# Nine 512-column strips of a hybrid diffusion layer, computed by seven quarter products

## The reference

```
h = modulate(rms_norm(x))                      # (tokens, 1024)
q, k, v, r = h@Wq, h@Wk, h@Wv, h@Wr            # widths 512, 512, 1024, 1024: gated linear attention (GLA)
o, _ = gla_chunked(q, k, v, decay, state)      # both directions, 4 heads
ya = (rms_norm(o) * silu(r)) @ gla_proj        # 1024 x 1024
yb = Re(DFT2(h @ Wu)) @ fnet_proj              # Fourier mixing
yc = ssd(...) @ ssd_proj                       # Mamba-2 branch, done before q
y  = sigmoid(h@Wga)*ya + sigmoid(h@Wgb)*yb + sigmoid(h@Wgc)*yc
x1 = x + gate * (y @ w_out);  then routed_moe(...)   # 16 experts, top 2
```

## Time and profile before

| | us |
|---|---|
| median of 3 timed runs | 1718.51 |
| lowest, highest | 1715.67, 1721.17 |
| span of the profiled execution | 1712.4 |
| PE busy in it | 1602.6 (94%) |
| DVE busy in it | 691.1 (40%) |
| ACT busy in it | 388.0 (23%) |

### The profile page before, as it was taken

The page is one execution under the profiler, slowest core; times in us unless marked ns, Lnnn a source line. Parts: engine busy times, 40 slices in busy tenths (PEclk is TensorE's granted clock), DMA queues, the critical chain, the costliest instruction groups (busy, mean ns, idle before and its releaser), DMA issues.

```text
span 1712.4 us, 23396 instructions
## 1 busy us (share of the span) xinstructions
PE 1602.6 (94%) x9120; PEld 872.7 (51%) x9121; DVE 691.1 (40%) x1281; ACT 388.0 (23%) x730; POOL 290.2 (17%) x311
## 2 busy tenths in 40 slices
PE   6999999999999899999999999999999979999893
PEld 3464564564554444445455554446575655555451
DVE  2445745745645746000167773033243232222224
ACT  4332432422432310000133334101110211111112
POOL 0006406407407400000000000000000032222222
PEclk9999999999999999999999999999999999999997
DMA  9802301311411574211111012126135269997994
GB/s 344 323 21 81 99 31 44 99 38 37 123 49 25 181 259 150 98 51 49 49 50 49 1 50 84 63 74 238 61 136 197 103 241 392 360 373 283 395 342 159
DMA packets 110339, 248.47 MB, mean 145 GB/s; under 512 B 5665, under 2 KB 15142, under 8 KB 110274
## 3 DMA queue, kind: packets, MB, share of 16 engines
q1 hardware_dynamic: 86800, 180.60, 29.4%
q0 software_dynamic: 14288, 48.96, 7.9%
q10 hardware_dynamic: 9186, 18.01, 3.7%
HBM read 225.40 MB, written 22.15 MB: 145 GB/s over the span
## 4 chain that ended last, share of the span: by engine, by line
PE 81%; DVE 9%; DMA 3%; ACT 2%; issue 2%; POOL 2%; ACTq 0%; DVEq 0%; POOLq 0%
PE psum L456 17%; PE psum L470 9%; PE psum L1152 9%; PE psum L803 6%; PE psum L669 5%; PE psum L1177 5%; PE psum L460 4%; DVE arena L1941 2%; PE psum L969 2%; PE psum L926 2%; PE psum L939 2%; PE psum L850 2%; PE psum L712 1%; PE psum L568 1%; PE psum L703 1%
## 5 line engine op out<-in xcount | busy, mean ns | idle before, releaser
L456 PE MATMUL psum<-arena 128*128 128x512 f32 x688 | 300.8, 593 | 1.3 <-DVE arena L1952 0.8
L456 PEld LDWEIGHTS psum<-arena 128*128 128x128 f32 x688 | 128.1, 189 | 157.4 <-issue 155.9
L1152 PE MATMUL psum<-arena 128*32 128x256 f32 x2816 | 164.5, 385 | 1.5 <-issue 1.0
L470 PE MATMUL psum<-arena 128*128 128x512 f32 x352 | 152.9, 593 | 1.6 <-issue 1.6
L1152 PEld LDWEIGHTS psum<-arena 128*32 128x32 f32 x2816 | 92.7, 110 | 57.9 <-issue 4.9
L669 PE MATMUL psum<-arena 128*128 128x512 f32 x256 | 118.4, 594 | 0.0
L803 PE MATMUL psum<-arena 128*128 128x512 f32 x256 | 111.5, 593 | 0.0
L470 PEld LDWEIGHTS psum<-arena 128*128 128x128 f32 x352 | 66.2, 190 | 81.5 <-issue 81.1
L2416 POOL TENSOR_TENSOR arena<-arena 128x512 f32<-128x512 f32 x64 | 89.3, 1416 | 35.7 <-ACT arena L1469 35.7
L1821 DVE SCALAR_TENSOR_TENSOR arena<-arena 128x772 f32<-128x772 f32 (+1 forms) x96 | 93.9, 978 | 3.4
L2378 POOL TENSOR_TENSOR arena<-arena 128x512 f32<-128x512 f32 x40 | 44.9, 1130 | 277.7 <-ACT arena L1402 270.3
(11 more groups left out here) (378 smaller groups left out, 2054.0 us busy)
## 6 DMA issues: line engine op xcount, KB each, us to landing
arena<-exp_w_d SPq DMA_DIRECT2D x48, 2048.0 KB, 16.9
arena<-w_in_d SPq DMA_DIRECT2D x22, 2048.0 KB, 8.0
arena<-ada_w_d POOLq DMA_DIRECT2D x8, 2048.0 KB, 10.1
slots<-arena POOLq DMA_DIRECT2D x1, 9216.0 KB, 26.7
arena<-ada_w_d SPq DMA_DIRECT2D x4, 2048.0 KB, 20.6
arena<-decay_rows ACTq DMA_DIRECT2D x16, 512.0 KB, 6.0
arena<-ssd_proj_d SPq DMA_DIRECT2D x4, 2048.0 KB, 11.2
slots<-arena POOLq DMA_DIRECT2D x92, 64.0 KB, 5.0
```

Source lines behind the costliest of these rows:

```text
L456: ins = mmul(ps[:, 0:T], slot[:, k, m * P:(m + 1) * P], src[:, k, C:NT], start=(k == 0), stop=(k == KD - 1))
L470: ins = mmul(ps[:, 0:n], src[:, k, t * P:(t + 1) * P], slot[:, k, 0:n], start=(k == 0), stop=(k == KD - 1))
L1152: ins = mmul(psU[q * R:(q + 1) * R, 0:2 * HF], XT[:, k % 2, k // 2, :], w13[p][:, :, k, q * HF:(q + 1) * HF], start=(k == 0), stop=(k == K ...
```

## The change

Nine of the strips (q, k, the latent rows of the first half of v, r in two, gla_proj in two, gb in two) are each seen as a 2 x 2 block product: 512 outputs as two column halves, 1024 inputs as two halves, 512 tokens as two halves. In place of eight products of quarters each strip forms seven (Strassen's scheme in Winograd's form): every one is 8 matmuls of 128x256 times 2, that is, 2 x 4 matmuls in the program and 16 records. The sums of token quarters T1 to T4 are made once for h (`hT_sums`, in the third place of the ring) and once for oT; the sums of weight quarters S1 to S4 are made for each strip by four DVE additions of 128x1024. Products 1 and 2 share the bank "a", 5 and 3 the bank "d", 6, 7 and 4 the bank "b"; between products of one bank partial results are read out: ACT copies product 1 (`p1_out`), DVE adds (`p16_out`, `p15_out`, `c22_out`, `c12_out`, `c21_out`), 128x512 each, and ACT writes the last quarter (`c11_out`). The context tokens of k and v stay eight-product work in matmuls of their own. While `hT_sums` occupies place 2, the ring has two places (`ways`), from ssd_proj to the second strip of gb. Some semaphores are merged under common names. The transfer of the position table moves from before the constants to behind the second strip of gb.

```diff
+            ways.remove(2)
+            strips.append([[], ("gb1", "b"), 2])
...
+            def seven_strip(name, slot, x, x_sums, w_sums, ready, tokens=False, lo=0, hi=8, order=(1, 6, 5, 7, 3, 4, 2), between=()):
...
+                def product(at, w, x, first, last):
+                    ps = bank((name, at))
+                    for i in range(2):
+                        for k in range(4):
+                            held, passed = (x, w) if tokens else (w, x)
+                            ins = mmul(ps[:, i * 256:(i + 1) * 256], held[:, k, i * P:(i + 1) * P], passed[:, k, :],
...
+                    elif p == 7:
+                        pe.wait_ge(S_("w_summed"), 4 * n + 3)
+                        pe.wait_ge(S_(ready[0]), ready[1][2])
+                        pe.wait_ge(S_("p16_out"), n + 1)
+                        product("b", S3, T3, False, False).then_inc(S_("part_made"), 1)
...
+                    elif p == 4:
+                        pe.wait_ge(S_("c22_out"), n + 1)
+                        pe.wait_ge(S_(ready[0]), ready[1][3])
...
             slot = full_strip(pe, w_in, Q0)
-            for m in range(4):
-                project_T(slot, m, hT, ("q", m))
-            strip_used(("q", 3))
+            seven_strip("q", slot, of_hT, hT_sums, early_sums[0:3], hT_ready, lo=2)
...
             slot = full_strip(pe, a["gla_proj"][0], 0)
...
+            seven_strip("pa0", slot, of_oT, oT_sums, late_sums, oT_ready, hi=4, order=(1, 5, 2, 3, 6, 7, 4),
+                        between=((1, turn_rest),))
...
+            gate_half(1)
+            ways.append(2)
...
             phase_end(act, 2)
             act.dma_start(rw, a["router_w"].rearrange("(k p) e -> p k e", p=P)).then_inc(S_("rw_in"), 16)
-            act.dma_start(pos2, a["pos"].rearrange("(t p) d -> p t d", p=P)).then_inc(S_("pos_in"), 16)
...
+            gb_out(1)
+            act.dma_start(pos2, a["pos"].rearrange("(t p) d -> p t d", p=P)).then_inc(S_("pos_in"), 16)
...
+            def sum_w(name, sums, i):
+
+                n, slot, landed = seven[name]
+                at = S_("w_summed")
+                if i == 0:
+                    dve.wait_ge(*landed)
+                    v.tensor_tensor(sums[0], cols_of(slot, 1, 0), cols_of(slot, 1, 1), ALU.add).then_inc(at, 1)
...
+            p16_out("pa0", late_tmp)
+            spare = zb[:, 0:512]
+            merge_11("pa0", spare, 0)
+            c12_out("pa0", late_tmp, by_half(late_tmp[1]))
+            dve.wait_ge(*is_free(("pa0", "d")))
+            merge(late_tmp[1], 0, 1, 0)
+            sums_w("pa1", late_sums)
+            c22_out("pa0", late_tmp, by_half(late_tmp[2]))
...
             v.memset(ho[:, :, 0:1], 0.0).then_inc(S_("h_folded"), 1)
...
+            gb_sums(0)
             for j in range(2):
                 slot, arrived, count = aside_at[("U", j)]
                 dve.wait_ge(arrived, count)
```

521 lines of the change are left out of this document (375 added, 146 removed).

## The result

The changed kernel takes 1696.7 us (median of 4 executions, 1691.9 to 1698.4) beside 1718.6 of the kernel before (4, 1715.7 to 1721.2): ratio 0.9888, 95% interval 0.9855 to 0.9921, 21.9 us less. The forecast was 10.2 less, the range ended at 1700. The sign was right; the gain is about twice as large, and the range did not hold it.

The account below looks back on a forecast made before the run. PE, busy 94% of the span, was taken as the bound. Strips -30.6, waits +17.9, a vanished ACT wait -0.5 and clock +3.0 gave -10.2 us: span 1712.4 to 1702.2, plus 6.1 to the median, 1708.3; range 1700 to 1714.

Parts of the forecast that it names:

- the seventh wait: Before the second pb product, for a bank freed after x lands and DVE adds positions and copies: 4.1 us.
- the step from span to median: Whole kernel: the profiled span lies 6.1 us under the timed median, and the same distance holds after the change.
- the fifth wait: Before product 7 of gb's first strip, for a DVE add behind ACT's queue of transfers and copy: 2.75 us.
- A strip saves 3.4, nine save 30.6: Nine strips on PE: seven products take 24.2 us in place of 27.6, saving 3.4 us each, 30.6 in all.
- rival (c): Strips on PE: weight loads make 128x256 records slower than 216 ns, so the kernel is slower, 1735 us; chance 0.05.
- VectorE's price and the default order: Each strip adds 8.6 us on DVE; in the default product order q, k, v, r and second strips don't wait.
- The ring of two: Weight strips with two places: a transfer lands after 8.0 us beside 24 us of the strip between, costing nothing.
- Waits 1 to 4: PE in gla_proj: first strip's x sums 0.25, product 7 1.0, product 4 5.85; second strip's product 1 0.95 us.
- Wait 3: Before product 4 of the first gla_proj strip, for c22 queued on DVE behind merges and four sums: 5.85 us.
- Wait 6, the U fold, 3.0: Before the U work after gb's first strip, for DVE's fold, which stands behind c21: 3.0 us.
- The clock, 3.0: PE at the lower clock after the waits of 5.85 and 4.1 us: 3.0 us together, with ends 0 and 6.0.
- Rival (a), the covers hold: Whole kernel: transfers come earlier, no wait for x, no clock fall; 17.3 us less, 1701; chance 0.22.

Follow-up runs that it names:

- gb1_by_eight: Changed kernel with gb's second strip back at eight products, without sums or read-outs of parts; 1699.1 us, ratio 0.9930.
- c22_first: Changed kernel with the first gla_proj strip's c22 read-out and merge on VectorE ahead of the next strip's four weight sums; 1690.7 us, ratio 0.9868.
- before_pos: Kernel before with the position table's transfer issued behind gb's sigmoids, ahead of x, not ahead of the DFT constants; ratio 0.9984.
- act_late: Changed kernel with five more 128x512 copies on ScalarE between its queue of transfers and the copy of gb's first product; 1701.9 us, ratio 0.9939.
- u_first: Changed kernel with the first U strip's fold on VectorE between two read-outs of gb's first strip, not behind the last; 1696.3 us, ratio 0.9898.
- x_late: Changed kernel with the x rows' transfer issued only after ScalarE has read the second of five fe banks; 1707.8 us, ratio 0.9963.
- before_bank: Kernel before with the first w_out block opening PSUM bank 4 in place of bank 2; ratio 0.9994.
- before_again: Kernel before, no edit, run once more for a second profile; its DFT part took 24.47 us.

## Why the prediction was right and wrong

The forecast was 1708.3 and the measurement 1696.7, 11.6 lower. The step that failed most is the seventh wait: its 4.1 us and the 1.5 us of clock with it rest on x landing 27.5 us after gb, and it landed at 22.1. Next come the step from span to median (5.2 us) and the fifth wait (2.75 us, put on 7.5 us of transfer issues that took 4.6). Against these stand a strip's gain put too high and a clock that fell where none was forecast. The mechanism (fewer records on PE, paid for by waits in VectorE's queue) was right.

First the sum over the columns that repeat (q to U, U to DFT, pb to wo), 17.2 us less, where the forecast had 10.2 for the whole.

- **A strip saves 3.4, nine save 30.6.** Right in kind: products run at 3.45 us and 24.15 to 24.4 a strip. gb1_by_eight gives 3.3; what is left of the 17.2 us once waits, clock and the bank are taken out gives 28.8 for nine, 3.2 each. 1.8 us too much. Part of that is in the measure: start to start, q, v and gb's second strip save 3.28, 3.24 and 3.30 (29.5 for nine), and a wait costs 0.2 to 0.3 us more start to start than the idle shown (1106.50 - 1097.70 - 3.45 = 5.35 for the 5.10). No rival (c): 1008 loads of 191 ns stand under matmuls 216 ns apart. The rule of the Trainium skill ("TensorE: Matmul & The Clock Gate", on what overlaps and what doesn't) that was weighed against this, a load overlapping only work in other row groups, is not what the trace shows.
- **VectorE's price and the default order.** Right: no wait in q, k, v, r, the second gla_proj strip and both gb strips beyond their first product. The ring of two cost nothing.
- **Waits 1 to 4.** 0.25, 1.0, 5.85, 0.95 forecast; 0, 0.94, 5.10, 0.90 measured. Wait 3 is shorter in part since the four sums took 4.7 us and not 5.0: those that don't depend on each other start 1.14 us apart, not 1.25. c22_first shows the cause of the wait. The 0.48 us at L926 went as forecast.
- **Wait 5, ScalarE's queue, 2.75.** Not there. The failed step is the 7.5 us for the transfer issues, taken from the earlier trace rows with only the moved transfer's own issue subtracted. They took 4.6, of which the table's absence explains 1.4 (before_pos) and the rest stays open; act_late shows that the chain behind them was right.
- **Wait 6, the U fold, 3.0.** 2.84, and u_first shows it.
- **Wait 7, x, 4.1.** Not there, and this is the largest miss. x landed 22.1 us after gb's end and not at 27.5. The forecast's own terms, 24.7 + 2 + 1.5, are 28.2, a slip of 0.7. The 24.7 took 340 GB/s from the earlier trace rows, a mean over 14 us that holds the start of the transfers, while this stretch runs at 386 to 407 (the row below has 407). 4.2 MB at half of 400 is 21 us, 3.7 less, which leaves about 1 us for beginning, evacuation and issue in place of 3.5. So the two queues did share about alike, which is what the Trainium skill's "DMA: Bandwidth & Descriptors" (section on queues, rings and completion order) has on queues. That they are served by issue is out: a w_out strip asked for at 1219.97 landed at 1243.5, behind the position table, asked for at 1223.01 on the other queue and landed at 1237.0. What was in flight in the earlier trace rows was misread, too: beside x a w_out strip, and the expert weight behind that. The second pb product wanted the bank at 32.0 and not at 28.75, since the DFT part ran partly at the lower clock (0.50 in the row below); but x at 22.1 frees it at 27.4, ahead of either. x_late shows the mechanism to be true.

```profile
1231.00:1234.00 3.00, 3.00 (x10) 1.32 (x10) 2.97 (x3) 0.59 (x1) 0.00 (x0) 0.50 1.03 407
```

- **The clock, 3.0.** Forecast 1.5 for each of waits 3 and 7 and nothing for wait 6. Measured 2.2 behind wait 3 and 1.75 behind wait 6, so 4.0. The earlier trace rows was one case of several: behind waits of 3.27 (act_late) and 5.04 us (x_late) it was 1.75 and 4.1.
- **What was not foreseen, 1.7.** The bank under w_out. The idle of 1.58 was in the earlier trace rows and was read only as a sample of the clock.

Waits give 8.1 us of the difference, wait 7's clock 1.5 and the bank 1.7; strips take back 1.8 and the clock of waits 3 and 6 takes 2.5: 7.0 together, which is 17.2 - 10.2.

**Beyond these columns.** The profiled span fell by 16.6 us, from 1712.4 to 1695.8, 6.4 more than forecast: the 7.0, less 3.2 that the DFT part took more than in the first profile of before, plus 2.6 that w_out to the end took less. Neither is a step of the forecast, and both columns move by as much for one kernel.

**From span to median.** The step "the same distance of 6.1 us holds" failed as well: the median after lies 0.9 us over the profiled span, not 6.1, and that is 5.2 us. In the 130 executions for which both numbers are listed, the time is 1.5 to 3.3 us over its own span. By that the profiled execution of before, whose own time isn't listed, took some 1714 to 1716 us, at or under the lowest of the timed ones; the distance compared a short execution with a median. With the 2.6 us of the changed kernel's profiled execution, the forecast's own span of 1702.2 would have read 1704.8, still outside the measurement. 6.4 and 5.2 are the 11.6.

Rival (a), the covers hold, came nearest in size and in mechanism, since wait 7 is gone. That its 17.3 less is the 17.2 found is luck: 4.0 us less of waits and 1.7 for the bank against 1.8 on the strips and 4.0 for two falls of the clock that it did not have.

## What to carry to other kernels

When a tuned engine list gets shorter on its busiest engine, put each result that the engine waits for ahead of work that nobody needs yet in the helper's queue, and look at which buffer it frees as well; with one bank opened elsewhere, that order was worth 13.5 us here, against 17.2 for the change itself. A duration read from a profile belongs to what was in flight beside it: when a transfer is moved away, read the issue times and rates again from a stretch without it. Compare stages between fixed points, and take a term from a single profile only when the stage repeats in a second one.

## What the runs showed of the hardware

- The granted clock fell to 0.50 amid work without any idle stretch (before_bank, 1243 to 1248) and stood at 1.00 in another execution over the same instructions. That makes 3 to 5 us in the DFT part. In the stage before q, where the times of one kernel spread by 5 us, the granted clock was 0.66 in one execution and 1.00 in another over the same 10 us.
- The same wait of 2.84 us is followed by the lower clock in five profiles (U work 29.70) and not in two (28.02), where an earlier wait had been filled with work or another had come 16 us ahead. 3.16 us (c22_first) were not followed by it, 3.27 (act_late) were. What decides is not shown.
- Issuing the same eleven transfers took ScalarE 4.5 to 5.6 us in the changed kernels, 6.1 in before_pos, and 7.5 (before) to 8.2 (before_again), the table's own issue taken off, with its transfer in flight.
- Two queues busy together moved 386 to 407 GB/s, and 4.2 MB on one of them took 22.1 us, near the half.
